# The second network's attention in shorter turns: turning and values of one unit share a turn with the scores of the unit two ahead

## The reference, cut to what matters

```python
def diff_attn(q, k, v, lam):
    s = jnp.einsum("bqhmd,bkhmd->bhmqk", q.astype(F32), k.astype(F32)) * (B_QK_DIM ** -0.5)
    p = jax.nn.softmax(s, axis=-1)
    a = p[:, :, 0] - lam * p[:, :, 1]
    return jnp.einsum("bhqk,bkhd->bqhd", a, v.astype(F32))
```

## Time and profile before

| what | value |
|---|---|
| median of three runs | 2413.66 us (2406.47 to 2415.41) |
| the profiled execution: its own time | 2416.61 us |
| its span from first to last instruction | 2415.0 us |
| PE busy | 2214.7 us, 92% |
| DVE busy | 1416.3 us, 59% |
| ACT busy | 1051.4 us, 44% |
| POOL busy | 306.3 us, 13% |
| mean granted clock of TensorE | 0.951 of full speed |
| attention units of the first layer | from 1481.04 us to about 1550 us |
| attention units of the second layer | from 2110.42 us to about 2154 us |

### The profile page before, as it was taken

How to read it: one execution, slowest core, us unless ns; L and a number is a source line. 1 busy time by engine, 2 the same in 40 slices (tenths; PEclk the granted TensorE clock), 3 DMA queues, 4 the chain that set the end, 5 groups by cost and what they waited for, 6 DMA issues and landing times. The chain is left out here.

```text
span 2415.0 us, 31203 instructions
## 1 busy us (share of the span) xinstructions
PE 2214.7 (92%) x11948; PEld 1797.3 (74%) x11948; DVE 1416.3 (59%) x2231; ACT 1051.4 (44%) x1745; POOL 306.3 (13%) x313
## 2 busy tenths in 40 slices
PE   8999899899999999898998987779999998778998
PEld 6777677678777777676887765568888886658987
DVE  4655485544456554854554698654655338766764
ACT  4445544444445455554444454522332225454442
POOL 0005421000000054220000171000000002400000
PEclk9999899999999989999999998789999999889999
DMA  7645334465656543344655321222332334234554
GB/s 234 203 165 163 118 122 141 147 214 191 221 191 208 167 166 123 131 144 172 220 181 179 112 69 53 71 63 98 104 129 88 121 98 148 61 115 140 192 175 148
DMA packets 171842, 349.28 MB, mean 145 GB/s; under 512 B 11824, under 2 KB 23216, under 8 KB 171696
## 3 DMA queue, kind: packets, MB, share of 16 engines
q1 hardware_dynamic: 171696, 347.29, 43.9%
HBM read 346.19 MB, written 1.05 MB: 144 GB/s over the span
## 5 line engine op out<-in xcount | busy, mean ns | idle before, releaser
L825 DVE TENSOR_TENSOR wlo<-wraw,whi 128x1024 fp32r<-128x1024 f32 (+1 forms) x535 | 646.0, 1220 | 704.4 <-ACT whi L1022 702.0
L1022 ACT ACTIVATE whi<-wraw 128x1024 fp32r<-128x1024 f32 (+1 forms) x552 | 557.8, 1027 | 600.1 <-PE psum L1779 279.2
L1779 PE MATMUL psum<-whi,act_h 128*128 128x512 f32 (+2 forms) x1424 | 576.2, 405 | 20.1 <-DVE wlo L825 8.2
L1779 PE MATMUL psum<-wlo,act_h 128*128 128x512 f32 (+2 forms) x1424 | 556.0, 390 | 0.0
L1779 PE MATMUL psum<-whi,act_l 128*128 128x512 f32 (+2 forms) x1424 | 555.2, 390 | 0.0
L1779 PEld LDWEIGHTS psum<-whi,act_h 128*128 128x128 f32 x1424 | 274.2, 193 | 88.3 <-issue 22.5
L1779 PEld LDWEIGHTS psum<-whi,act_l 128*128 128x128 f32 x1424 | 273.1, 192 | 57.3
L1779 PEld LDWEIGHTS psum<-wlo,act_h 128*128 128x128 f32 x1424 | 274.2, 193 | 48.9
L1779 PE MATMUL psum<-act_h,whi 128*128 128x512 f32 (+1 forms) x704 | 243.8, 346 | 15.3 <-DVE cacc L1400 6.3
L1779 PE MATMUL psum<-act_l,whi 128*128 128x512 f32 (+1 forms) x704 | 239.7, 340 | 0.0
L1779 PE MATMUL psum<-act_h,wlo 128*128 128x512 f32 (+1 forms) x704 | 239.0, 340 | 0.0
(11 more groups left out here) (268 smaller groups left out, 2759.0 us busy)
## 6 DMA issues: line engine op xcount, KB each, us to landing
wraw<-in_w_in SPq DMA_DIRECT2D x136, 512.0 KB, 4.3
wraw<-in_w_gate SPq DMA_DIRECT2D x104, 512.0 KB, 4.1
wraw<-in_w_mod_pieces SPq DMA_DIRECT2D x96, 512.0 KB, 4.8
wraw<-in_w_ffn_in SPq DMA_DIRECT2D x80, 512.0 KB, 4.5
wraw<-in_w_ffn_out SPq DMA_DIRECT2D x44, 512.0 KB, 4.5
wraw<-in_w_down SPq DMA_DIRECT2D x44, 512.0 KB, 4.3
wraw<-in_w_val SPq DMA_DIRECT2D x40, 512.0 KB, 4.3
wraw<-in_w_branch SPq DMA_DIRECT2D x32, 512.0 KB, 4.8
```

The costliest lines, as they stand in the source:

```text
L825: eng.tensor_tensor(wlo[:, i, 0:st.n, 0:st.w], wraw[:, st.s % RING_W, 0:st.n, 0:st.w], whi[:, i, 0:st.n, 0:st.w].bitcast(F32), ALU.subtrac ...
L1022: nc.scalar.activation(whi[:, d % RING_S, 0:st.n, 0:st.w], wraw[:, s % RING_W, 0:st.n, 0:st.w], ACT.Copy).then_inc(sem("slab_rounded"), 1)
L1779: return nc.tensor.matmul(out, lhsT, rhs, start=start, stop=stop)
```

## The change

Only the two lines that write the turns are changed:

```diff
         pl.turns = (0, 1)
-        for i in range(len(units) + 3):
-            for kind, u in (("att2_s", i), ("att2_v", i - 3), ("att2_t", i - 2), ("att2_e", i), ("att2_m", i - 1)):
+        for i in range(len(units) + 2):
+            for kind, u in (("att2_t", i - 2), ("att2_s", i), ("att2_e", i), ("att2_m", i - 1), ("att2_v", i - 2)):
                 if not 0 <= u < len(units):
                     continue
```

## The result

The changed kernel takes 2429.49 us (median of 8 executions, 2420.99 to 2434.65), the kernel before, timed beside it, 2413.52 us (8 executions, 2406.47 to 2418.86). The ratio is 1.0071, 95% interval 1.0051 to 1.0090: 12 to 22 us slower by the interval, 16.0 by the two medians. The forecast was 2432, range 2421 to 2442.

The account below looks back on a forecast made before the run. Steady turns were taken as bounded by PE and DVE work, some 3 us, then by a 4.48 us loop. 8.5 + 7 + 3 = 18.5 us on 2416.61 gave 2435.1 profiled, 2432 in the median, range 2421 to 2442.

Parts of the forecast that it names:

- Steady turns bounded by work, now by a loop of 4.48 us: Full-width attention turns: some 3 us of PE and DVE work becomes a loop of scores, maxima, mix, turning, scores, 4.48 us.
- First layer, units 0 to 6: First layer's attention, mix of unit 0 to mix of unit 6: 31.4 us instead of 23.74, a loss of 7.7 us.
- Units 7 to 15: First layer's 256-wide units: lag of the mix between 7.5 and 9.3 us, 8.5 us for the layer at full clock.
- Second layer: Second layer's attention: 28.3 us instead of 20.5 up to the mix of unit 5, a loss of 7 us at the last mix.
- The clock, +3: Turns of both attention stretches running at 1.2 GHz: 0 to +14 us possible, a quarter taken, +3 us.
- Everything outside is equal: Outside the two attention stretches, about 9 to 12 and 7 to 9 us longer, the profile would show no change.
- Clock low throughout: Rival: the clock falls through both attention stretches, +12 in place of +3, 2441 us (2438 to 2446); chance 0.12.
- Mostly covered: Rival: evictions, gate additions and scaling fill DVE's gap, only 6 pure turns lose 1.5 us each, about 2423; chance 0.15.
- Not slower: Rival: the removed turn saves some 3 us in each layer's drain if the mix is over before PE's turning, 2408; chance 0.05.

Follow-up runs that it names:

- e2: Changed kernel with the scores of unit i put back ahead of the turning of unit i-2 on PE; 2413.51 us, ratio 1.0012 to the kernel before.
- e7: Changed kernel with the mix of unit i-1 moved ahead of the maxima of unit i on DVE; 2420.13 us, ratio 1.0050 to the kernel before.
- a1: Changed kernel, unchanged, profiled again; attention stretches 75.00 and 46.08 us, span 2424.4 us.
- b1: Kernel before, unchanged, in a third profile; attention stretches 61.70 and 38.12 us, span 2413.6 us.
- e1: Kernel before with only the turning moved ahead of the scores, values and eviction of i-3 left ahead of the mix; 2461.1 us, ratio 1.0207.
- e5: e1 with the values and eviction of unit i-3 moved behind the mix; 2431.65 us, ratio 1.0092 to the kernel before.
- e4: Changed kernel with, on PE alone, stream pieces between a turning and scores moved behind those scores; 2431.52 us, ratio 1.0094 to the kernel before.
- e0: Kernel before, unchanged, timed and profiled again; ratio 1.0010, attention stretches 63.23 and 38.13 us.

## Why the prediction was right

**Steady turns bounded by work, now by a loop of 4.48 us: right.** Turns without a piece in them take 4.46, 4.46 and 4.47; the two of 4.80 and 4.91 hold a gate addition between maxima and mix, or a stream piece between turning and scores. Inside it the turning to the scores took 0.59 us and not 0.53, the scores to the maxima 1.15 and not 1.24. DVE's maxima were to wait 1.3 to 1.6 us in nearly every turn. They did so in two, 1.54 and 1.54. Before these it was 2.99 (unit 2, with PE at the lower clock), after them 0.56 (behind a gate addition that itself waited 1.00) and 1.08. For unit 7 they didn't wait, since two copies (L1540, 1.28 us) filled the gap on DVE, and the turn was still 4.47 long. e2 shows that the order of turning and scores on PE closes it, e7 that the maxima ahead of the mix are in it.

**First layer, units 0 to 6: right**, 31.4 us forecast and 31.4 measured. **Units 7 to 15: too small.** The loss should have moved between 7.5 and 9.3 us and ended at 8.5. It is 9.1 to 10.3 for units 7 to 11, 11.1 at unit 12 and 10.9 at the last mix (71.6 against 60.7); in a1 the last mix is at 73.3, since PE did the values beside the mix of unit 7 (2.08 us against 1.16), and later another product (at 1546.01, 1.15 against 0.71), at 1.2 GHz. The half-width turns go on waiting: the maxima at 1517.35, 1532.81 and 1536.60 waited 1.11, 0.43 and 1.27 us for scores. The slab wait did shorten, from 3.46 to 2.25 us, 1.2 and not 1.5. How the remaining 2.4 us divide among the half-width turns was not taken apart.

**Second layer: too small by 1.4.** 8.4 us at the last mix, not 7; at the mix of unit 5 30.6, not 28.3. I counted one stream piece in the line at full clock; a second stands between a turning and scores, behind a wait, at the lower clock. Timeline of PE, changed kernel:

```profile
2131.51 1.11 PE L1782 MATMUL psum<-ident,e 128*128 128x128 f32 x4 [2.73 <-DVE e L1484]
2132.55 1.08 PE L1779 MATMUL psum<-wraw,condm 128*32 128x128 f32 x16
2133.56 1.80 PE L1779 MATMUL psum<-kT,qT 64*128 64x512 f32 x4
```

From the start of this turning to the maxima (2135.40) it takes 3.89 us, where the loop had 0.53 + 1.24 = 1.77 (the one piece that I did count stands in the first turn). That is 2.1 of the 2.3 us by which the sum up to unit 5 was short. At full clock the same three take 0.59, 0.58 and 1.15, together 2.32 us (rows above, the piece by b1's row in the last section). So 0.6 of the 2.1 is the piece that I hadn't counted, and some 1.5 is the lower clock: a part of what the clock term stood for is in this number.

**The clock, +3: no general fall, but single turns.** The mean granted clock of the stretches didn't fall, it rose by 0.01 to 0.04. In the full-width turns only some of those behind a long wait ran at 1.2 GHz, as above, and what that cost is inside the two layer terms. The three terms together were 8.5 + 7 + 3 = 18.5; the stretches of the first profile show 10.1 + 8.0 = 18.0, of which the clock term is no separate part. So the sum came out through two terms too small and one that has no part of its own, and that it came within half a microsecond is in part luck. By the means of three profiles the stretches cost 19.6, and the whole time 16.0 by the medians. "Everything outside is equal" was seen to 2.4 us and no finer. The full-width stretch at clock 0.94 had idles of PE of 0.6 to 1.5 us in its turns of 4.5 to 4.9 and kept the higher level. The rule of the Trainium skill weighed in the prediction ("TensorE: Matmul & The Clock Gate", section "A second HAM failure mode: psum-queue depth-cycling"), that short idles between groups of matmuls can make the clock alternate, did not come true there. In the half-width turns the clock does go between its two levels (scores of 0.70 and of 1.23 us, mean 0.76), but it did so before the change as well (0.72), so that is not the change's doing. e1's half-width turns, with mixes 6.2 us apart on average, had 0.61; what in them did that was not isolated.

**The rivals.** "Clock low throughout" is refuted by the windows. "Mostly covered" is refuted: no full-width turn was shortened by what fills the gap. "Not slower" asked for the mix ahead of the maxima; e7 did that and was still 1.0050, because the wait for the exponentials closes a loop of 4.25 us. That rival's condition was put too simply: it looked at one loop only.

## What to carry to other kernels

In a software pipeline over in-order engines, walk every cycle: an instruction that waits for another engine holds up all behind it, so what feeds that engine next must be issued ahead of the wait. Here the scores of i ahead of the turning of i-2 is worth some 15 us, and the number of turns saved is worth nothing that could be told. Where a loop can't be avoided, put whatever isn't in it (here the eviction) behind the instruction that closes it, on every engine that has a part in it: e5 against e1 is 26 us, of which an unknown part is the clock, and e4 shows that moving a piece on one engine alone gains nothing. And opening one loop leaves the next one (e7): work out the second before promising the gain.

## What was not expected of the hardware

The moment at which the clock returns to 2.4 GHz differs between executions of the same code. The same piece of TensorE work, first in the profile of before and then in b1:

```profile
1486.67 1.08 PE L1782 MATMUL psum<-ident,e 128*128 128x128 f32 x4 [0.24 <-DVE e L1484]
1487.68 1.08 PE L1779 MATMUL psum<-wraw,condm 128*32 128x128 f32 x16
1488.69 1.83 PE L1779 MATMUL psum<-kT,qT 64*128 64x512 f32 x4
```
```profile
1489.47 0.66 PE L1782 MATMUL psum<-ident,e 128*128 128x128 f32 x4 [0.24 <-DVE e L1484]
1490.06 0.64 PE L1779 MATMUL psum<-wraw,condm 128*32 128x128 f32 x16
1490.64 1.13 PE L1779 MATMUL psum<-kT,qT 64*128 64x512 f32 x4
```

The three take 3.85 us in one and 2.30 in the other, which is the 1.5 us by which b1's first stretch is shorter. Such steps bound what one profile can say of a stretch (1.5 to 1.7 us here, a1 against the first profile of the changed kernel). The head of the program, with 13 us of scatter, bounds what it can say of the whole. Here too it is TensorE that takes longer for the same work: for the same 7268 matmuls up to the first scores it was busy 1366.3 us in e0, 1373.5 in the profile of before and 1376.5 in b1, while these scores start at 1470.62, 1481.04 and 1483.85. So 10.2 us of the 13.2 are busy time of PE. The whole time of the changed kernel moves with the mean granted clock, from 2420.99 us at 0.959 to 2434.65 at 0.951.
